# First recurrence: the inverse of each chunk's triangular matrix, worked on as its two 32x32 diagonal blocks

## The reference, cut to what matters

```python
    def step(S, inp):
        r_t, w_t, k_t, v_t, a_t, b_t = inp
        sa = jnp.einsum('bhvk,bhk->bhv', S, a_t)
        S = S * w_t[:, :, None, :] + sa[..., None] * b_t[:, :, None, :] + v_t[..., None] * k_t[:, :, None, :]
        return S, jnp.einsum('bhvk,bhk->bhv', S, r_t)
```

## Time and profile before

| | |
|---|---|
| Median of three runs | 2186.79 us (2184.38 to 2191.1) |
| The profiled execution | 2187.91 us, of which its span, first to last instruction, is 2186.1 us |
| TensorE matmul (PE) busy | 2094.6 us, 96% of the span |
| Weight load (PEld) | 1665.9 us, 76% |
| VectorE (DVE) | 1238.5 us, 57% |
| ScalarE (ACT) | 812.9 us, 37% |
| GpSimd (POOL) | 262.2 us, 12% |
| Mean granted TensorE clock | 0.986 of full speed |

### The profile page before, as it was taken

One profiled execution on the slowest core, in us unless ns is written; L12 is line 12 of the kernel. 1 busy time (PEld: TensorE's weight loads), 2 busy tenths in 40 slices (PEclk: granted clock), 3 DMA queues, 4 the chain that ended last, 5 costly groups with the idle time before them and its releaser, 6 DMA issues. The chain is left out here.

```text
span 2186.1 us, 30854 instructions
## 1 busy us (share of the span) xinstructions
PE 2094.6 (96%) x12664; PEld 1665.9 (76%) x12664; DVE 1238.5 (57%) x1692; ACT 812.9 (37%) x1268; POOL 262.2 (12%) x266
## 2 busy tenths in 40 slices
PE   8899989999999999999999999999998999999996
PEld 6776867788878778888777888877665577888885
DVE  5547866642343576766563454457768638533544
ACT  4344223631332434444362322334234554222321
POOL 0000002000001100000100880020652010000002
PEclk9999999999999999999999999999999999999998
DMA  6220003222322132222123222224211042233221
GB/s 231 67 67 32 4 3 106 87 97 97 97 97 87 58 97 77 68 78 68 49 97 101 87 97 97 97 82 129 69 58 35 2 145 87 88 89 112 97 80 65
DMA packets 51676, 179.24 MB, mean 82 GB/s; under 512 B 5784, under 2 KB 5784, under 8 KB 51280
## 3 DMA queue, kind: packets, MB, share of 16 engines
q1 hardware_dynamic: 47712, 165.45, 23.3%
q10 hardware_dynamic: 3328, 8.13, 1.0%
q0 software_dynamic: 496, 3.69, 0.4%
HBM read 172.51 MB, written 4.21 MB: 81 GB/s over the span
## 5 line engine op out<-in xcount | busy, mean ns | idle before, releaser
L1150 DVE TENSOR_TENSOR w_lo<-w_raw,w_hi 128x1024 fp32r<-128x1024 f32 (+1 forms) x320 | 413.1, 1293 | 713.5 <-ACT w_hi L1143 713.2
L1248 PE MATMUL banks<-xh,w_hi 128*128 128x512 f32 x1560 | 625.1, 401 | 4.6 <-PEq L214 3.6
L1250 PE MATMUL banks<-xh,w_lo 128*128 128x512 f32 x1560 | 610.2, 391 | 0.0
L1249 PE MATMUL banks<-xl,w_hi 128*128 128x512 f32 x1560 | 609.9, 391 | 0.0
L1143 ACT ACTIVATE w_hi<-w_raw 128x1024 fp32r<-128x1024 f32 (+1 forms) x320 | 328.5, 1029 | 713.0 <-PE banks L1250 675.4
L1248 PEld LDWEIGHTS banks<-xh,w_hi 128*128 128x128 f32 x1560 | 294.7, 189 | 75.7 <-issue 14.6
L1250 PEld LDWEIGHTS banks<-xh,w_lo 128*128 128x128 f32 x1560 | 294.0, 188 | 63.1
L1249 PEld LDWEIGHTS banks<-xl,w_hi 128*128 128x128 f32 x1560 | 294.7, 189 | 58.7 <-issue 1.7
L1248 PE MATMUL banks<-hh,w_hi 128*128 128x512 f32 x688 | 270.5, 393 | 5.6 <-PEq L214 4.3
L1249 PE MATMUL banks<-hl,w_hi 128*128 128x512 f32 x688 | 268.4, 390 | 0.0
L1250 PE MATMUL banks<-hh,w_lo 128*128 128x512 f32 x688 | 268.3, 390 | 0.0
(11 more groups left out here) (513 smaller groups left out, 2555.3 us busy)
## 6 DMA issues: line engine op xcount, KB each, us to landing
w_raw<-in_w SPq DMA_DIRECT2D x128, 512.0 KB, 3.4
w_raw<-in_w_gu SPq DMA_DIRECT2D x44, 512.0 KB, 3.4
w_raw<-in_w_c_in SPq DMA_DIRECT2D x40, 512.0 KB, 3.4
w_raw<-in_w_ab_in SPq DMA_DIRECT2D x27, 512.0 KB, 3.5
w_raw<-in_w_in SPq DMA_DIRECT2D x25, 512.0 KB, 3.4
w_raw<-in_w_down SPq DMA_DIRECT2D x16, 384.0 KB, 3.1
w_raw<-in_w_down SPq DMA_DIRECT2D x16, 320.0 KB, 2.8
w_raw<-in_w_ab_out SPq DMA_DIRECT2D x8, 512.0 KB, 3.5
```

Source lines behind the costliest of these rows:

```text
L1150: dve.tensor_tensor(lo[:, 0:n], core.raw[u % RAW][:, 0:n], hi[:, 0:n].bitcast(F32), ALU.subtract).then_inc(core.split_ready, 1)
L1248: pe.matmul(bank, hi[:, w], src.xh[:, kk, :], start=kk == 0, stop=False)
L1249: pe.matmul(bank, hi[:, w], src.xl[:, kk, :], start=False, stop=False)
L1250: mm = pe.matmul(bank, lo[:, w], src.xh[:, kk, :], start=False, stop=last)
```

## The change

The inverse of a 64x64 unit triangular matrix has two 32x32 inverses on its diagonal and one corner block. The change keeps only the two diagonal blocks through the first five levels (sizes 1 to 16), packed side by side: a group of X is now `[P, 2, 4, 32]`, 128 partitions by 256 columns, where each block keeps its own 32 partitions. A call of TensorE is then a 32x32 tile (32 partitions in, 32 columns of weights, 32 moving columns, 32 partitions out), and `quarters` lists 32 calls where `in_chunk` lists 16.

- X and X^T of 32-blocks are tiles of their own, X in `Y[:, 4:6]`, X^T in `Y[:, 6:8]`. GpSimd fills X with unit blocks when the stage starts.
- The first level is made by TensorE and VectorE: N's diagonal blocks times the unit (32 calls a group, behind `tok(5)`), copied into X under the mask of level 0, then transposed. The mask, addition and transposes in the pair phase go.
- Levels 1 to 4 are 16 steps, each with a question and a product of 32 calls. VectorE's mask, sum and transpose are 128x256. The transpose is now made in every step. Products wait for the sum of two steps before and the transpose of four before.
- The last level makes the corner in TensorE: `diagonal` turns the blocks into the full X^T in a PSUM bank and fills its fourth block with zeros, `corner_questions` multiplies N's corner by X, ScalarE copies it, `corner_products` multiplies by X^T into the bank, and ScalarE copies the whole X^T (128x512) to its place in `Y`. `answers_in` then waits for that copy.
- ScalarE gets eight copies, four 128x256 and four 128x512.

The diff, cut to its core. Removed lines are those of the kernel above: the loops over `n` of VectorE, `level_products` and the loop over levels of TensorE.

```diff
-        Nt, X, XT = grouped(kk), grouped(k), grouped(Y[:, 0:4, :])
+        Nt, XT = grouped(kk), grouped(Y[:, 0:4, :])
...
+        quarters = [(b, m, e, i) for b in range(2) for m in range(4) for i in range(2) for e in range(2)]
+        packed = lambda bank: core.psum[bank][:, 0:256].rearrange("p (b m t) -> p b m t", b=2, t=32)
+        of_unit = lambda b, m: slice((4 * b + m) * 32, (4 * b + m + 1) * 32)
...
+        def pool(gp):
+            gp.tensor_copy(X[:].rearrange("p g b m t -> p (g b m) t"),
+                           eye.rearrange("p (o t) -> p o t", o=1).broadcast_to([P, 32, 32])).then_inc(s.units, 1)
...
+            def corner(g):
+                act.wait_ge(s.corner, g + 1)
+                if g > 1:
+                    act.wait_ge(s.xt_ready, g - 1)
+                act.activation(corners[:, g % 2], packed(Q_BANK[g % 2]), ACT.Copy).then_inc(s.corner_out, 1)
...
+            def inverse_out(g):
+                act.wait_ge(s.xt_ready, g + 1)
+                act.activation(XT[:, groups[g][0], groups[g][1]], in_group(FULL_BANK[g]), ACT.Copy).then_inc(s.xt_out, 1)
...
-                    dve.wait_ge(s.masked, 2 * p + 1)
-                    dve.tensor_tensor(XT[:, a_, h], Nt[:, a_, h], lvl("lmask", 0), ALU.mult).then_inc(s.x_level, 1)
-                    dve.wait_ge(s.x_level, 2 * g + 1)
-                    dve.tensor_tensor(XT[:, a_, h], XT[:, a_, h], lvl("lmask", 6), ALU.add).then_inc(s.x_level, 1)
...
-                    dve.tensor_tensor(Q[:, c % 2], in_group(Q_BANK[c % 2]), lvl("lmaskt", l), ALU.mult).then_inc(s.q_out, 1)
...
+            def turn(n):
+                g = (n - 1) % 4
+                dve.wait_ge(s.x_sum, n)
+                dve.transpose(rows(XT32[:, g]), rows(X[:, g])).then_inc(s.x_turned, 1)
+
+            def add(n):
+                g = (n - 1) % 4
+                dve.wait_ge(s.x_prod, n - 4)
+                dve.tensor_tensor(X[:, g], X[:, g], packed(X_BANK[g % 2]), ALU.add).then_inc(s.x_sum, 1)
+                turn(n)
+
+            for n in range(1, 21):
+                l, g = divmod(n - 1, 4)
+                dve.wait_ge(s.q_ready, n)
+                if l == 0:
+                    if n == 1:
+                        dve.wait_ge(s.units, 1)
+                    dve.copy_predicated(X[:, g], within(0).bitcast(mybir.dt.uint32).broadcast_to([P, 2, 4, 32]), packed(X_FROM[g])).then_inc(s.x_sum, 1)
+                    turn(n)
+                else:
+                    if n > 6:
+                        dve.wait_ge(s.x_prod, n - 6)
+                    dve.tensor_tensor(Q32[:, g % 2], packed(Q_BANK[g % 2]), within(l).broadcast_to([P, 2, 4, 32]), ALU.mult).then_inc(s.q_out, 1)
+                if n > 5:
+                    add(n - 1)
+            add(20)
...
+            for n in range(1, 5):
+                a_, h = groups[n - 1]
+                pe.wait_ge(s.masked, 14 if n < 3 else 16)
+                for b, m, e, i in quarters:
+                    at_ = quarter(e ^ b, i)
+                    mm = pe.matmul(core.psum[X_FROM[n - 1]][at_, of_unit(b, m)], Nt[at_, a_, h, b, m, 32 * i:32 * i + 32], eye[at_],
+                                   start=True, stop=True)
+                mm.then_inc(s.q_ready, 1)
...
+            def level_products(n):
+                g = (n - 1) % 4
+                pe.wait_ge(s.x_sum, n - 2)
+                pe.wait_ge(s.q_out, n - 4)
+                pe.wait_ge(s.x_turned, n - 4)
+                for b, m, e, i in quarters:
+                    at_ = quarter(e ^ b, i)
+                    mm = pe.matmul(core.psum[X_BANK[g % 2]][at_, of_unit(b, m)], XT32[at_, g, b, m], Q32[at_, g % 2, b, m], start=True, stop=True)
+                mm.then_inc(s.x_prod, 1)
...
+            def level_questions(n):
+                g = (n - 1) % 4
                 a_, h = groups[g]
+                if n < 7:
+                    pe.wait_ge(s.tok_out, 8)
+                else:
+                    pe.wait_ge(s.q_out, n - 6)
+                pe.wait_ge(s.x_sum, n - 4)
+                for b, m, e, i in quarters:
+                    at_ = quarter(e ^ b, i)
+                    mm = pe.matmul(core.psum[Q_BANK[g % 2]][at_, of_unit(b, m)], Nt[at_, a_, h, b, m, 32 * i:32 * i + 32], X[at_, g, b, m],
+                                   start=True, stop=True)
+                mm.then_inc(s.q_ready, 1)
...
+            def diagonal(g):
+
+                pe.wait_ge(s.x_turned, 17 + g)
+                bank = core.psum[FULL_BANK[g]]
+                for b, m, e, i in quarters:
+                    at_ = quarter(e ^ b, i)
+                    pe.matmul(bank[at_, half_at(b, m, i)], eye[at_], XT32[at_, g, b, m], start=True, stop=True)
+                for e in range(2):
+                    at_ = quarter(e, 1)
+                    pe.matmul(bank[at_].rearrange("p (n t) -> p n t", t=C)[:, :, 0:32], core.mask("spare")[at_, 0:32],
+                              core.mask("spare")[at_, 32:288].rearrange("p (n t) -> p n t", t=32), start=True, stop=True)
+
+            def corner_questions(g):
+                a_, h = groups[g]
+                pe.wait_ge(s.q_out, min(15 + g, 16))
+                if g > 1:
+                    pe.wait_ge(s.corner_out, g - 1)
                 for b, m, e in in_chunk:
+                    mm = pe.matmul(core.psum[Q_BANK[g % 2]][quarter(e ^ b, 1), of_unit(b, m)], Nt[quarter(e ^ b, 0), a_, h, b, m, 32:64],
+                                   X[quarter(e ^ b, 0), g, b, m], start=True, stop=True)
+                mm.then_inc(s.corner, 1)
+
+            def corner_products(g):
+                pe.wait_ge(s.corner_out, g + 1)
+                for b, m, e in in_chunk:
+                    mm = pe.matmul(core.psum[FULL_BANK[g]][quarter(e ^ b, 0), half_at(b, m, 1)], corners[quarter(e ^ b, 1), g % 2, b, m],
+                                   XT32[quarter(e ^ b, 1), g, b, m], start=True, stop=True)
+                mm.then_inc(s.xt_ready, 1)
+
+            def answers_in(g):
+                a_, h = groups[g]
+                pe.wait_ge(s.xt_out, g + 1)
...
+            for n in range(5, 21):
+                level_questions(n)
+                if n > 5:
+                    level_products(n - 1)
+                if n in (6, 8):
+                    values_in(n // 2 - 1)
+            diagonal(0)
+            corner_questions(0)
+            level_products(20)
+            for g in range(1, 4):
+                diagonal(g)
+                corner_questions(g)
+                corner_products(g - 1)
+            answers_in(0)
+            corner_products(3)
+            for g in range(1, 4):
+                answers_in(g)
```

More of the change, by code:

```diff
@@ L103, in const_array @@
     a["lmask"][:] = both(np.concatenate(levels + [s == t], 1))
-    a["lmaskt"][:] = both(np.concatenate([m.T for m in levels], 1))
+    a["pmask"][:, 0:160] = np.concatenate([np.tile(m.T[0:32, 0:32], (4, 1)) for m in levels[0:5]], 1)
     m = a["sel"].reshape(P, 4, P)
@@ L1362, in rwkv @@
         bt, kt, bonus = chunked(a), chunked(k), O[:, 0:4, :]
-        Nt, X, XT = grouped(kk), grouped(k), grouped(Y[:, 0:4, :])
+        Nt, XT = grouped(kk), grouped(Y[:, 0:4, :])
+        quarter = lambda e, i: slice(64 * e + 32 * i, 64 * e + 32 * i + 32)
+        Q32 = [ap.rearrange("p q b t -> p (q b t)").rearrange("p (x b m t) -> p x b m t", x=2, b=2, t=32) for ap in (Q[:, 0], Q[:, 1])]
+        Q32, corners = Q32
         Arb, Aak, Ark = grouped(lw), grouped(a), grouped(r)
         s = st.sems("bonus_ready shifted gated gate_scaled const_ready "
-                    "tok tok_out pairs masked x_level x_first "
-                    "q_ready q_out x_prod x_sum x_turned "
+                    "tok tok_out pairs masked units "
+                    "q_ready q_out x_prod x_sum x_turned corner corner_out xt_ready xt_out "
                     "d_ready d_out xd_ready xd_out a_ready a_out sa_ready sa_out h_ready h_out start_ready states_in y_ready y_out "
@@ L1422, in _, with answers_out @@
                 act.activation(Aak[:, groups[c][0], groups[c][1]], in_group(D_BANKS[c]), ACT.Copy).then_inc(s.d_out, 1)
-            for c in range(4):
-                act.wait_ge(s.xd_ready, c + 1)
-                act.activation(Aak[:, groups[c][0], groups[c][1]], in_group(XD_BANKS[c]), ACT.Copy).then_inc(s.xd_out, 1)
+            def corner(g):
[6 more added lines that the diff above has]
+                act.activation(XT[:, groups[g][0], groups[g][1]], in_group(FULL_BANK[g]), ACT.Copy).then_inc(s.xt_out, 1)
+            def answers_out(g):
+                act.wait_ge(s.xd_ready, g + 1)
+                act.activation(Aak[:, groups[g][0], groups[g][1]], in_group(XD_BANKS[g]), ACT.Copy).then_inc(s.xd_out, 1)
+            corner(0)
+            corner(1)
+            inverse_out(0)
+            corner(2)
+            inverse_out(1)
+            corner(3)
+            inverse_out(2)
+            answers_out(0)
+            inverse_out(3)
+            for g in range(1, 4):
+                answers_out(g)
             def answer(n):
```

(13 more changed lines are left out.)

58 lines of the change are left out of this document (11 added, 47 removed).

## The result

The changed kernel took 2227.76 us, median of five runs (2225.77 to 2229.08), against 2186.78 us in five runs of the kernel before on the same chip (2183.42 to 2191.1): a ratio of 1.0183, 95% interval [1.0172, 1.0195]. It is 41 us slower. The forecast was 2224, with a range of 2212 to 2240. The profiled execution took 2228.44 us, its span 2226.7.

A forecast was written before the change was run, and what follows sets the result against it. Bound: TensorE's instruction supply, 256 per 3.46 us. 27.7 blocks make 95.8 us, 37.3 over 58.45; plus 0.5 for a copy, less 0.8 for masks, gives 2224.9 against the profiled execution, 2224 against the median; range 2212 to 2240.

The forecast's parts named there:

- Supply decides: Inverse stage: TensorE's instructions arrive in blocks of 256, about 3.46 us apart; 27.7 blocks, +37.3 us; given 83%.
- the prediction's sign of a dependency: Stops in the stage at unit boundaries behind VectorE or ScalarE would show the supply forecast wrong.
- Pairs and packets: TensorE's weight-load-and-matmul pairs rise from 12,664 to 14,208, instruction packets from 101 to about 113.
- The block's interval, 3.46 us: Time per 256-instruction block in the 32x32 part, 127 pairs each; allowed 3.35 (+34.3 us) to 3.95 (+51).
- three windows of 3.45 to 3.48 us: Four-tile code of the kernel before, read as standing still a third of the time, so faster tiles hardly shorten them.
- Clock, taken as 0 of 0 to 5: Idle TensorE may be granted 1.2 GHz, slowing answers and the recurrence's first part: 0 to 5 us, 0 likeliest.
- The stage's end: The last answers move from 291.1 to about 328 us.
- The recurrence, taken as unchanged: Everything after the answers keeps its pairs; stretches behind 330 us should match before's, shifted.
- The last inverse copy, +0.5 us: ScalarE's last 128x512 copy of the whole inverse, ahead of the answers, may show: 0 to 2 us, 0.5 taken.
- VectorE's saving, valued at nothing: Smaller masks, sums and transposes save over 20 us of VectorE, hidden inside the block interval.
- One and two: In the stage: blocks hidden, VectorE sets the pace, 2172, 8%; 14.6 ns a pair, no supply limit, 2187, 4%.
- Three: In the stage, a pair costs 29.2 ns whatever its tile: +44 us, 2232, evenly spaced without stops; 5%.

The follow-up runs named there:

- runs that leave calls, tiles and VectorE alone: Changed kernel reading only the upper 16 bits, one pair a call: in level questions and products, 2200.19 us; in every 32x32 unit, 2188.47 us.
- the runs at full clock: Changed kernel with 39 useless 128x512 matmuls added, 2232.25 us; or with one replacing the last call of each level question, 2225.76 us.
- the run with full clock up to the answers: Changed kernel with 39 useless float32 128x512 matmuls, 31 beside level units and 8 beside diagonals and corner questions: 2232.25 us.
- the kernel before with one pass: Kernel before, level questions and products reading only the upper 16 bits of their float32 words, 640 pairs fewer: 2180.56 us, ratio 0.9954.
- 10 us put back: Changed kernel with two more 128x256 masks for VectorE per level question, into a scratch tile nobody reads: 2228.24 us, ratio 1.018.
- the run with the early slow matmul: Changed kernel with one useless float32 128x512 matmul in place of the last call of each level question: 2225.76 us, ratio 1.0175.

## Why the forecast held, and where it was off

- *Supply decides.* Right. The stops are where they were forecast, 127 pairs apart, and the time follows the number of blocks in runs that leave calls, tiles and VectorE alone (-28.9 us for 8 blocks, -40.3 for 11, where -27.7 and -38.1 were forecast). One of the 26 stops, that at 314.15 us, is labelled as a wait for VectorE's transpose, which would be the prediction's sign of a dependency; but the transpose that those calls need, the seventeenth, had ended at 306.57, and the stop comes 3.57 us behind the one before, so supply fits it too. By the Trainium skill's page "Runtime: NRT & Kernel Launch", section "Instruction fetch mechanics", the crossing should have been mostly hidden; in the six windows above 1.65 us or more stood open at each crossing.
- *Pairs and packets.* As forecast: 14,208 and 113.
- *The block's interval, 3.46 us.* Mis-sized. From 233.62 to 328.72 us there are 3309 pairs and some 40 separate waits, 26 blocks, and 95.10 / 26 = 3.66 us, since some last 3.7 to 4.03. That is +5.1 us. I had allowed 3.35 to 3.95. The prediction read its three windows of 3.45 to 3.48 us as standing still for a third of the time; by their rows TensorE was busy 2.72, 3.23 and 2.35 us, so it stood for a fifth, and for a third in one of them. Its own range also falls 3 us short of its parts: 2186.8 + 51 and 5 for the clock are 2243, not 2240. The forecast doesn't hang on either.
  The trace shows where the longer blocks come from. Count from a stop to the packet, and from the packet to the next stop's end. In most blocks of the levels these are 1.0 to 1.2 and 2.3 to 2.5 us. In the two of 4.03 us the packet starts 1.6 to 1.7 us behind the stop and the rest is 2.4 as ever, though no wait was added there:

```profile
DMA  0000000000000000500000000000000000000000
```

  (289.27 to 293.30 us in 40 slices; the packet is in the 17th.) In the ones of 4.0 us from 237.63 to 249.63 the packet is as early as elsewhere (1.0 to 1.1), and the next block comes 2.9 to 3.0 us behind it. In the two-tile blocks of the kernel before, 3.96 and 4.03 us long, it is 1.4 and 2.6. What sets either part stays open.
- *Clock, taken as 0 of 0 to 5.* +2.3 us, all of it in the answers; the steps are untouched, as the runs at full clock show.
- *The stage's end*: 328 forecast, 337.1 measured. The 9 us are these two and 1.3 us ahead of the stage, all but some 0.4.
- *The recurrence, taken as unchanged.* 4.0 us shorter, which gave back nearly half of that error in the total. In the kernel before two stops of 1.72 and 1.94 us stand in its first 12 us, and now the longest there is 0.76:

```profile
297.69 0.21 PEld L1751 LDWEIGHTS banks<-Z,rwkv_tokV 64*64 64x64 f32 x8 [1.72 <-issue]
...
302.39 0.24 PEld L1711 LDWEIGHTS banks<-Y,rwkv_tokA 64*64 64x64 f32 x9 [1.94 <-issue]
```

```profile
344.55 0.26 PEld L1797 LDWEIGHTS banks<-Y,rwkv_tokA 64*64 64x64 f32 x11 [0.60 <-issue]
347.22 0.32 PEld L1837 LDWEIGHTS banks<-Z,rwkv_tokV 64*64 64x64 f32 x16 [0.76 <-issue]
```

  Why blocks are ready sooner there now is open. Two causes lie near, and other runs show that neither is needed for most of it. TensorE had just spent 6 us on slow answers; but in the run with full clock up to the answers (3.9 us) the recurrence still takes 30.0 us from its first weight load to its last squares (338.69 to 368.70), against 29.6 in the changed kernel and 33.6 before. And the boundaries fall about 16 instructions elsewhere; but in the kernel before with one pass, whose queue is shorter by just 5 blocks (1280 instructions), the stops fall at the same calls as before (0.44 and 1.66 us in place of 1.72 and 1.94), and it takes 30.9 us, behind answers of 5.2 us. The forecast of 2224 was thus nearer than its parts, by luck: an error of 9 us in the stage met one of 4 us the other way that nobody had counted.
- *The last inverse copy, +0.5 us.* Not seen: corner products run to 332.62 us and the answers go on at 332.69.
- *VectorE's saving, valued at nothing.* Right (22 us less work in the span, none of it in the time; 10 us put back, no change).
- *Rivals.* One and two (2172, 2187) are out by the total. Three (29.2 ns a pair whatever the tile, 2232) lay near the measured time and only the profile refutes it: 64 pairs of a product unit start within 0.61 us at full clock (293.56 to 294.17 in the run with the early slow matmul), 9.5 ns each, and then TensorE stands. That is also well under the 25 ns between starts of the Trainium skill's page "TensorE: Matmul & The Clock Gate", section "Wait — 56ns, not 53.3ns?".

## What to carry to other kernels

Where matmuls are so small that 256 instructions of TensorE run in less than the 3.4 to 4.0 us that a block took here, count instructions, not columns or VectorE's work: splitting a tile into four quarters made the calls faster and the program slower. Look for "issue" in the middle of a loop, cut the trace there, and see whether equal counts of instructions lie between the cuts. Where they did, fewer passes a call saved time, and less work for VectorE did not. A microsecond of slow work put into each such stop cost nothing here.

## What was not expected of the hardware

- A separate wait on TensorE's queue that is long met costs about 0.1 us. Sixteen of them in the first part of a block, in place of four calls, made the block longer (3.95 us on average), while a slow matmul of about a microsecond in the same place did not (3.63 us, as without it). The next packet starts 1.0 to 1.2 us behind a stop in most blocks of dense matmuls and 1.5 to 1.8 us with waits. A front end that takes instructions ahead of the matmuls but halts at waits would do this; that reading was not tested, and it doesn't account for the blocks of the changed kernel in which the packet starts 1.6 us behind the stop without such waits.
- The interval of a block is not one number: 3.43 to 3.48, 3.76 and 4.03 us stand side by side in the same loop of the same execution, with the same instructions.
- TensorE was granted half clock (0.50) from 275 to 329 us, though it worked in every block; one matmul of 128x512 at the end of each question kept it at 1.00 from 256 to 290 us and 0.94 from there to 322.
